# Summing the residual's squares on GpSimd instead of TensorE, for the first token block of each stage boundary

## The chip, the cores and the metric

The kernel runs on one core of one Trainium2 chip. Its metric is the device time of one execution in microseconds. Times of engines come from one profiled execution.

## The reference, cut to what matters

A decoder trunk of two layers over 1040 tokens (16 meta tokens and 1024 real ones), 1024 channels wide: a Mamba-2 mixer with a convolutional feed-forward network, then sliding-window attention over shared keys and values with another such network. Each of the four parts is normed before and after, and added to the residual stream `h`:

```python
def rms_norm(x, w):
    xf = x.astype(jnp.float32)
    y = xf * lax.rsqrt(jnp.mean(xf * xf, axis=-1, keepdims=True) + RMS_EPS)
    return (y * w.astype(jnp.float32)).astype(x.dtype)

for i in range(DEPTH):
    if i < N_A_LAYERS:
        mix = mamba2_mixer(rms_norm(h, a_norm_pre[j]), ...)
        h = h + rms_norm(mix, a_norm_post[j])
    else:
        if j == 0:
            kv = (rms_norm(h, kv_norm) @ w_kv).reshape(...)
        mix = swa_sink_attention(rms_norm(h, b_norm_pre[j]), ...)
        h = h + rms_norm(mix, b_norm_post[j])
    ffn = conv_ffn(rms_norm(h, f_norm_pre[i]), ...)
    h = h + rms_norm(ffn, f_norm_post[i])
```

The change bears on the mean of squares `mean(xf * xf)` of `h` in three of these norms.

## The kernel before, in words

All activations stay on chip, channels on the 128 partitions (8 groups of channels, index `k` or `m`), tokens along the free dimension. The 1040 tokens are cut in three blocks, `BLK`: block 0 with 272 tokens, blocks 1 and 2 with 384. Every projection is done with weights split in a high and a low fp16 half, three matmuls for each product (L1799 to L1801). Weights come through a buffer `stage`; ScalarE makes their high half (`hi`, L691), VectorE the low half (`lo`, L1258), and TensorE waits for `w_lo`.

Between two stages stands a *boundary* `p`: the last tiles of one projection, the post-norm, the addition to `h`, the pre-norm and the first tiles of the next projection overlap, block by block, in the order `ORD = (1, 2, 0)`; the first, second and third block below are meant in this order. Boundary 0 is after the Mamba-2 mixer, 1 after the first feed-forward network, 2 after attention, 3 at the end. `TAIL = (4, 2, 4, 2)` says how many of the 8 output tiles are done block by block, as *tail tiles*. There is no scheduler: each engine has one program written by hand, executed in order, and counting semaphores join them.

The squares of the mixer's output are summed over the 8 channel groups by GpSimd in `T2` (`tail_squares`, L595 the square, L617 the addition, a drain behind each), all but the last tile's, which ScalarE squares into `T1` once `T2` is done (it waits for `mix_sq_summed`; L884 in boundary 0, L886 in the others). TensorE turns the two into a mean over the channels by two products with a matrix of ones (`mean_post`, L1870 and L1872). ScalarE takes the reciprocal root (`rms`, L711 logarithm, L713 exponential), VectorE scales the output and adds it to `h` (`post`, L1274 and L1279, for each `k`), and ScalarE squares the new `h` (`square`, L727, semaphore `h_sq`). The sum over the 8 groups is done here by TensorE with eight accumulating products with ones (`mean_pre`, L1885). ScalarE's `pre` waits for all eight (`h_sq_used`), and VectorE's `pre` (L1292) then makes the normed input of the next projection, whose low halves (L358) are VectorE's and for two of the eight groups GpSimd's (`lows`).

The queues matter. GpSimd in a boundary does the tail squares of the first block, those of the second, the lows of the first, the tail squares of the third, the other lows. ScalarE with four tail tiles (boundaries 0 and 2) has this order, where `close(o1, ...)` ends with the square that waits for GpSimd:

```python
post(p, o0)
squares(q_, o0)
close(o1, tiles[1:])
pre(q_, o0)
```

With two tail tiles (boundary 1) `close(o1, tiles[1:])` comes after `pre(q_, o0)` and the first block's splits. TensorE in boundaries 0 and 2: the first block's tail tiles, one of the second block, `mean_post` of the first, the other three of the second, `mean_pre` of the first, two tail tiles of the third block, `mean_post` of the second, two more tail tiles, then the first two tiles of the next projection for the first block, `mean_pre` of the second, `mean_post` of the third, and the third tile of the next projection.

Of the kernel before, what the change touches and what calls it, by code (L numbers as in the profile page):

```python
# [7 lines left out]
KD = D // P  # L8
# [66 lines left out]
def first_slot(g):  # L75

    return GT + SLOTS * g
# [22 lines left out]
ORD = (1, 2, 0)  # L100
# [4 lines left out]
def block_rank(v, b):  # L105

    return b if v == 0 else ORD.index(b)
# [16 lines left out]
def program(nc, h0, wa, wd, wdt, prm, out):  # L124
    F32, F16 = mybir.dt.float32, mybir.dt.float16
    ALU, ACT, AX = mybir.AluOpType, mybir.ActivationFunctionType, mybir.AxisListType
    ds = bass.ds

    with ExitStack() as ctx:
        def sb(name, shape, dt=F32):  # L130
            return ctx.enter_context(nc.sbuf_tensor(name, shape, dt))

        def sem(name):
            return ctx.enter_context(nc.semaphore(name))
# [14 lines left out]
        onesD = sb("onesD", [P, P])  # L149
# [7 lines left out]
        PS = ctx.enter_context(nc.psum_tensor("PS", [P, 8, 512], F32))  # L157
# [5 lines left out]
        def mix_r1(k, b):  # L163
            s, n = BLK[b]
            return R1[:, ds(k * n + KD * s, n)]
# [14 lines left out]
        def mix_big(k, b):  # L180
            s, n = BLK[b]
            return BIG[:, k, s:s + n]
# [14 lines left out]
        def sq_slot(q, k, b):  # L197

            n = BLK[b][1]
            return AUX[:, 384 * k:384 * k + n] if q == 0 else mix_big(k, b) if q == 3 else mix_r1(k, b)  # L200
# [84 lines left out]
        update_ready, h_new = sem("update_ready"), sem("h_new")  # L285

        h_sq, h_sq_used, pre_rsqrt = sem("h_sq"), sem("h_sq_used"), sem("pre_rsqrt")
        x_normed, xn_hi, xn_lo_v = sem("x_normed"), sem("xn_hi"), sem("xn_lo_v")
        xn_lo_p = sem("xn_lo_p")

# [195 lines left out]
        def _(eng):  # L486
# [98 lines left out]
            def post_squares(p, j0, mix):  # L585
# [34 lines left out]

                return tail_squares

            def boundary(p, q, j0, mix):
                tail_squares = post_squares(p, j0, mix)
                tail_squares(ORD[0])
                tail_squares(ORD[1])
                if q is not None:
                    lows(q, ORD[0])
                tail_squares(ORD[2])
                if q is not None:  # L630
                    lows(q, ORD[1])
                    lows(q, ORD[2])
# [51 lines left out]
        def _(eng):  # L684
# [47 lines left out]

            def pre(q, b):
                s, n = BLK[b]
                eng.wait_ge(h_sq_used, 24 * q + 8 * block_rank(q, b) + 8)
                rms(T1, 2 if q == 0 and b == 1 else 7, s, n, pre_rsqrt, eps)

            def high(v, b, k):
# [243 lines left out]
            for g in range(NG - 1):  # L982
                for s in range(SLOTS):
                    i = first_slot(g) + s
# [26 lines left out]
            for s in range(SLOTS):  # L1011
                i = T_Z3 + s
# [168 lines left out]
            for c, (i, b) in enumerate(Q_SEQ):  # L1181
                s, n = BLK[b]
                eng.wait_ge(acc_ready, 3 * J_Q + c + 1)
                for hh in range(2):
                    r = eng.activation(q_stack(2 * i + hh, s, s + n)[64 * hh:64 * hh + 64],
                                       PS[64 * hh:64 * hh + 64, c % 6, 0:n], ACT.Copy,
                                       scale=1.0 / (WS * AD ** 0.5))
# [604 lines left out]
        def _(eng):  # L1792
# [81 lines left out]
            def mean_pre(q, b):  # L1874

                s, n = BLK[b]
                bank = 2 if q == 0 and b == 1 else 7
                if q == 0 and b == 2:
                    eng.wait_ge(pre_rsqrt, 1)
                elif q > 0:  # L1880
                    eng.wait_ge(pre_rsqrt, 3 * q + ORD.index(b))
                for k in range(KD):
                    i = 24 * q + 8 * block_rank(q, b) + k
                    eng.wait_ge(h_sq, i + 1)
                    eng.matmul(PS[:, bank, 0:n], onesD[:, :], sq_slot(q, k, b), start=(k == 0),  # L1885
                               stop=(k == KD - 1)).then_inc(h_sq_used, 1)

            def boundary(p, q, u0, j0, units, x, u_next, j_next, head_free=None):

# [218 lines left out]
            for g in range(NG):  # L2108
                for s in range(SLOTS):
                    i = first_slot(g) + s  # L2110
# [66 lines left out]
            for c, (i, b) in enumerate(Q_SEQ):  # L2177
# [5 lines left out]
                for k in range(KD):  # L2183
                    if i == 0:
                        wait_low(eng, x_index(3, b, k))
                    r = products(PS[:, c % 6, 0:BLK[b][1]], i % 2, k, x_big, b, k == 0, k == KD - 1)
# [147 lines left out]
```

## Time and profile before

| | us |
|---|---|
| median of 3 runs | 2694.93 (2693.72 to 2696.7) |
| the profiled execution | 2693.99 |
| its span | 2692.3 |
| TensorE busy | 2617.8 (97%) |
| VectorE busy | 1474.7 (55%) |
| ScalarE busy | 946.1 (35%) |
| GpSimd busy | 644.2 (24%) |

In the profile PE is TensorE (PEld its weight loads), DVE VectorE, ACT ScalarE, POOL GpSimd; `POOLq` is GpSimd's sequencer at a semaphore. L1885 is line 1885 of the kernel before. Busy shares are of the whole span, and a busy TensorE need not be on the path: what counts in a boundary is which wait ends last. Starts of matmuls are exact, their ends modelled, and a row of n merged instructions carries their common length. A product with ones of fp32 operands appears as two matmul records. The boundaries with the change lie at 830 to 905 us (0), 1541 to 1620 (1) and 1937 to 2016 (2).

### The profile page before, as it was taken

To read this page: it belongs to the slowest core of one execution; us is meant where nothing else is said; L and a number is where in the kernel's file an instruction comes from. 1 tells how busy PE (TensorE), PEld (TensorE's weight loads), DVE (VectorE), ACT (ScalarE), POOL (GpSimd) and SP (SyncE) were. 2 spreads that over 40 slices of the span, in tenths; PEclk is the share of its full clock that TensorE was granted. 3 is DMA by queue.
4 is the path that set the end of the run, shared out by engine and by line. 5 is a ranking of instruction groups with operands and counts; after the bars stand their busy time and mean duration, and the time that the engine had idled before them with its cause. 6 is when DMAs were issued, how large, how long until landed. Compare 5 with 4: busy or idle time off the path is not lost.

```text
span 2692.3 us, 43939 instructions
## 1 busy us (share of the span) xinstructions
PE 2617.8 (97%) x17942; PEld 1760.4 (65%) x17942; DVE 1474.7 (55%) x1898; ACT 946.1 (35%) x1742; POOL 644.2 (24%) x410
## 2 busy tenths in 40 slices
PE   8799999999999999999999998999999999999998
PEld 5566666666666666666666665676666666666665
DVE  6576676677587754544511267496276554543123
ACT  5333333343233423233211255497353223232121
POOL 1042544444234101100021211054421001001121
PEclk9899999999999999999999998998999999999999
DMA  3111111111131111111111111100111111111111
GB/s 110 39 32 40 32 40 32 32 36 36 32 119 32 40 55 47 50 52 47 59 51 54 48 32 32 48 2 2 47 32 55 49 52 47 54 50 54 54 54 63
DMA packets 38041, 123.93 MB, mean 46 GB/s; under 512 B 3361, under 2 KB 12705, under 8 KB 37921
## 3 DMA queue, kind: packets, MB, share of 16 engines
q1 hardware_dynamic: 37920, 122.25, 14.1%
q8 instruction: 86, 1.41, 0.2%
q14 instruction: 35, 0.28, 0.0%
HBM read 118.04 MB, written 4.19 MB: 45 GB/s over the span
## 4 chain that ended last, share of the span: by engine, by line
PE 87%; DVE 6%; ACT 4%; issue 2%; ACTq 1%; POOL 1%; POOLq 0%; DVEq 0%; DMA 0%
PE PS L1799 25%; PE PS L1800 25%; PE PS L1801 25%; PE PS L2016 2%; PE PS L1885 2%; ACT BIG L1198 1%; PE PS L2023 1%; PE PS L2046 1%; PE PS L2008 1%; DVE UB L1292 1%; ACT BIG L1211 1%; PE PS L2034 1%; PE PS L2066 1%; DVE BIG L1543 1%; DVE TT L1364 0%
## 5 line engine op out<-in xcount | busy, mean ns | idle before, releaser
L1799 PE MATMUL PS<-R,whi 128*128 128x384 f16 (+1 forms) x3168 | 987.0, 312 | 15.3 <-DVE wlo L1258 12.6
L1800 PE MATMUL PS<-R,whi 128*128 128x384 f16 (+1 forms) x3168 | 986.7, 311 | 0.0
L1801 PE MATMUL PS<-R,wlo 128*128 128x384 f16 (+1 forms) x3168 | 986.5, 311 | 0.0
L1258 DVE SCALAR_TENSOR_TENSOR wlo<-stage,whi 128x1024 f16<-128x1024 f32 (+1 forms) x182 | 246.1, 1354 | 733.8 <-ACT whi L691 733.7
L1799 PE MATMUL PS<-BIG,whi 128*128 128x384 f16 (+1 forms) x1452 | 452.2, 311 | 12.2 <-issue 8.3
L1800 PE MATMUL PS<-BIG,whi 128*128 128x384 f16 (+1 forms) x1452 | 452.3, 312 | 0.0
L1801 PE MATMUL PS<-BIG,wlo 128*128 128x384 f16 (+1 forms) x1452 | 452.2, 311 | 0.0
L1799 PEld LDWEIGHTS PS<-R,whi 128*128 128x128 f16 x3168 | 311.2, 98 | 180.1 <-issue 12.9
L1800 PEld LDWEIGHTS PS<-R,whi 128*128 128x128 f16 x3168 | 311.1, 98 | 162.5 <-issue 9.2
L1801 PEld LDWEIGHTS PS<-R,wlo 128*128 128x128 f16 x3168 | 311.2, 98 | 157.1 <-issue 1.0
L638 POOL TENSOR_TENSOR BIG<-TT,BIG 128x1040 f32 x44 | 96.7, 2197 | 799.9 <-ACT BIG L1113 799.9
L691 ACT ACTIVATE whi<-stage 128x1024 f16<-128x1024 f32 (+1 forms) x182 | 199.3, 1097 | 145.8 <-PE PS L1801 138.9
L1354 DVE SCALAR_TENSOR_TENSOR TT<-UB,pr,TT 128x1040 f32<-128x1040 f32 x168 | 218.7, 1302 | 29.3 <-issue 28.0
L521 POOL TENSOR_TENSOR TT<-AUX,upper 128x1024 f16<-128x1024 f16 (+1 forms) x72 | 154.7, 2169 | 256.3 <-PE PS L2046 229.4
L1799 PEld LDWEIGHTS PS<-BIG,whi 128*128 128x128 f16 x1452 | 142.6, 98 | 87.4 <-issue 13.0
L1800 PEld LDWEIGHTS PS<-BIG,whi 128*128 128x128 f16 x1452 | 142.5, 98 | 72.9 <-issue 3.9
L1801 PEld LDWEIGHTS PS<-BIG,wlo 128*128 128x128 f16 x1452 | 142.5, 98 | 72.2 <-issue 1.4
L785 ACT ACTIVATE UB<-PS 128x384 f32<-128x384 f32 (+1 forms) x120 | 54.8, 458 | 285.9 <-PE PS L1801 285.6
L1113 ACT ACTIVATE BIG<-TT 128x1040 f32 (+1 forms) x44 | 47.1, 1070 | 285.8 <-DVE TT L1678 285.8
L595 POOL TENSOR_TENSOR TT<-R 128x384 f32<-128x384 f32 (+1 forms) x63 | 51.3, 831 | 397.9 <-ACT R L705 260.3
L1364 DVE SCALAR_TENSOR_TENSOR TT<-UB,pr,TT 128x1040 f32<-128x1040 f32 x72 | 102.2, 1420 | 73.6 <-ACT TT L793 69.9
L705 ACT ACTIVATE UB<-PS 128x384 f32<-128x384 f32 (+1 forms) x240 | 99.8, 450 | 106.5 <-PE PS L1801 106.5
(240 smaller groups left out, 3189.4 us busy)
## 6 DMA issues: line engine op xcount, KB each, us to landing
stage<-wa SPq DMA_DIRECT2D x164, 512.0 KB, 3.5
stage<-wd SPq DMA_DIRECT2D x32, 704.0 KB, 4.0
hT<-h SPq DMA_DIRECT2D x4, 1536.0 KB, 11.2
out<-hT SPq DMA_DIRECT2D x4, 768.0 KB, 3.9
hT<-h SPq DMA_DIRECT2D x2, 1088.0 KB, 9.9
out<-hT SPq DMA_DIRECT2D x2, 512.0 KB, 2.8
pr<-prm SPq DMA_DIRECT2D x1, 328.0 KB, 6.6
BIG<-wdt SPq DMA_DIRECT2D x1, 128.0 KB, 10.6
```

What stands on the lines that cost most here:

```text
L521: r = eng.tensor_tensor(aU[part][0:T, 0:HG * T].rearrange("p (h l) -> p h l", h=HG), ar_p[part][0:T, ds(g * HG + c * NH, HG)].unsqueeze(2) ...
L638: eng.tensor_tensor(BIGh[:, ds(t, 1), L:2 * L], T2, BIGh[:, ds(t, 1), 0:L], ALU.subtract).then_inc(hid_lo, 1)
L691: eng.activation(WH[slot + 2 * aux][:, 0:width], stage[:, slot, 0:width], ACT.Copy, scale=WS).then_inc(w_hi, 1)
L705: r = eng.activation(dst, PS[:, 3 * st_ + b, 0:n], ACT.Copy, scale=scale)
L785: eng.activation(dst, PS[:, gemm_bank(i, b), 0:n], ACT.Copy, scale=scale).then_inc(evac, 1)
L1258: eng.scalar_tensor_tensor(out=WL[d][:, 0:width], in0=stage[:, slot, 0:width], scalar=WS, in1=WH[d][:, 0:width], op0=ALU.mult, op1=ALU.sub ...
L1354: r = eng.scalar_tensor_tensor(out=dst, in0=cin[:, o:o + L], scalar=prc(col + k), in1=dst, op0=ALU.mult, op1=ALU.add)
L1364: r = eng.scalar_tensor_tensor(out=T0, in0=UB[:, i % 2, o:o + L], scalar=prc(C_AW + (g * GT + j) * CONV_A + k), in1=T0, op0=ALU.mult, op1= ...
L1799: eng.matmul(acc, WH[slot][:, ws], x(0, k, b), start=first, stop=False)
L1800: eng.matmul(acc, WH[slot][:, ws], x(1, k, b), start=False, stop=False)
L1801: return eng.matmul(acc, WL[slot][:, ws], x(0, k, b), start=False, stop=last)
L1885: eng.matmul(PS[:, bank, 0:n], onesD[:, :], sq_slot(q, k, b), start=(k == 0), stop=(k == KD - 1)).then_inc(h_sq_used, 1)
```

## The change

GpSimd gets `residual_squares`, between the tail squares of the first and of the second block, in boundaries 0, 1 and 2. It adds the eight squares of `h` of the first block in two groups of four, each as a tree: two pair additions, a drain, one addition of the pairs' sums. TensorE then takes two products with ones for that block, where it took eight, and waits for `h_sq_sum`. For the second and third block, and for the kernel's first norm, the eight products stay. The semaphore `h_sq_used` counts one for each block after the first norm, and eight for each block in it.

```diff
--- before.py
+++ after.py
@@ -285,6 +285,7 @@
         update_ready, h_new = sem("update_ready"), sem("h_new")
 
         h_sq, h_sq_used, pre_rsqrt = sem("h_sq"), sem("h_sq_used"), sem("pre_rsqrt")
+        h_sq_sum = sem("h_sq_sum")
         x_normed, xn_hi, xn_lo_v = sem("x_normed"), sem("xn_hi"), sem("xn_lo_v")
         xn_lo_p = sem("xn_lo_p")
 
@@ -620,9 +621,23 @@
 
                 return tail_squares
 
+            def residual_squares(q_, b):
+
+                i = 24 * q_ + 8 * ORD.index(b)
+                for half in range(2):
+                    k0 = 4 * half
+                    for k in (k0, k0 + 2):
+                        eng.wait_ge(h_sq, i + k + 2)
+                        eng.tensor_tensor(sq_slot(q_, k, b), sq_slot(q_, k, b), sq_slot(q_, k + 1, b), ALU.add)
+                    eng.drain()
+                    eng.tensor_tensor(sq_slot(q_, k0, b), sq_slot(q_, k0, b), sq_slot(q_, k0 + 2, b),
+                                      ALU.add).then_inc(h_sq_sum, 1)
+
             def boundary(p, q, j0, mix):
                 tail_squares = post_squares(p, j0, mix)
                 tail_squares(ORD[0])
+                if q is not None:
+                    residual_squares(p + 1, ORD[0])
                 tail_squares(ORD[1])
                 if q is not None:
                     lows(q, ORD[0])
@@ -732,7 +747,7 @@
 
             def pre(q, b):
                 s, n = BLK[b]
-                eng.wait_ge(h_sq_used, 24 * q + 8 * block_rank(q, b) + 8)
+                eng.wait_ge(h_sq_used, 8 * (b + 1) if q == 0 else 24 + 3 * (q - 1) + ORD.index(b) + 1)
                 rms(T1, 2 if q == 0 and b == 1 else 7, s, n, pre_rsqrt, eps)
 
             def high(v, b, k):
@@ -1879,11 +1894,18 @@
                     eng.wait_ge(pre_rsqrt, 1)
                 elif q > 0:
                     eng.wait_ge(pre_rsqrt, 3 * q + ORD.index(b))
-                for k in range(KD):
-                    i = 24 * q + 8 * block_rank(q, b) + k
-                    eng.wait_ge(h_sq, i + 1)
-                    eng.matmul(PS[:, bank, 0:n], onesD[:, :], sq_slot(q, k, b), start=(k == 0),
-                               stop=(k == KD - 1)).then_inc(h_sq_used, 1)
+                summed = q > 0 and b == ORD[0]
+                ks = (0, 4) if summed else range(KD)
+                for k in ks:
+                    if summed:
+                        eng.wait_ge(h_sq_sum, 2 * (q - 1) + k // 4 + 1)
+                    else:
+                        eng.wait_ge(h_sq, 24 * q + 8 * block_rank(q, b) + k + 1)
+                    r = eng.matmul(PS[:, bank, 0:n], onesD[:, :], sq_slot(q, k, b), start=(k == 0), stop=(k == ks[-1]))
+                    if q == 0:
+                        r.then_inc(h_sq_used, 1)
+                if q > 0:
+                    r.then_inc(h_sq_used, 1)
 
             def boundary(p, q, u0, j0, units, x, u_next, j_next, head_free=None):
 
```

Order on GpSimd, boundary 0, before: `R` holds the mixer's output and the squares of `h`, `TT` the temporaries `T1` and `T2`. The rows are the last tail tile of the first block, the second block's three, and the first block's lows.

```order
L595 TENSOR_TENSOR TT<-R 128x384 [waits out_b]
L617 TENSOR_TENSOR TT<-TT 128x384
L595 TENSOR_TENSOR TT<-R 128x384 [waits out_b]
L617 TENSOR_TENSOR TT<-TT 128x384
L595 TENSOR_TENSOR TT<-R 128x384 [waits out_b]
L617 TENSOR_TENSOR TT<-TT 128x384
L595 TENSOR_TENSOR TT<-R 128x384 [waits out_b]
L617 TENSOR_TENSOR TT<-TT 128x384
L358 TENSOR_TENSOR R<-BIG,R 128x384 [waits xn_hi] x2
```

The same place after the change (L596 and L618 are the former L595 and L617):

```order
L596 TENSOR_TENSOR TT<-R 128x384 [waits out_b]
L618 TENSOR_TENSOR TT<-TT 128x384
L631 TENSOR_TENSOR R<-R 128x384 [waits h_sq] x2
L633 TENSOR_TENSOR R<-R 128x384
L631 TENSOR_TENSOR R<-R 128x384 [waits h_sq] x2
L633 TENSOR_TENSOR R<-R 128x384
L596 TENSOR_TENSOR TT<-R 128x384 [waits out_b]
L618 TENSOR_TENSOR TT<-TT 128x384
L596 TENSOR_TENSOR TT<-R 128x384 [waits out_b]
L618 TENSOR_TENSOR TT<-TT 128x384
L596 TENSOR_TENSOR TT<-R 128x384 [waits out_b]
L618 TENSOR_TENSOR TT<-TT 128x384
```

Six additions, the first four of which wait for ScalarE's squares of `h`, now stand ahead of the second block's three tail tiles.

TensorE, boundary 0, before: the end of the second block's tail tiles, the first block's products with ones (`onesD`), and the first tail tile of the third block.

```order
L1799 MATMUL PS<-BIG,whi 128x384
L1800 MATMUL PS<-BIG,whi 128x384
L1801 MATMUL PS<-BIG,wlo 128x384
L1885 MATMUL PS<-R,onesD 128x384 [waits h_sq,pre_rsqrt]
L1885 MATMUL PS<-R,onesD 128x384 [waits h_sq] x7
L1799 MATMUL PS<-BIG,AUX 128x272 [waits w_lo,out_b]
```

And after the change:

```order
L1814 MATMUL PS<-BIG,whi 128x384
L1815 MATMUL PS<-BIG,whi 128x384
L1816 MATMUL PS<-BIG,wlo 128x384
L1904 MATMUL PS<-R,onesD 128x384 [waits h_sq_sum,pre_rsqrt]
L1904 MATMUL PS<-R,onesD 128x384 [waits h_sq_sum]
L1814 MATMUL PS<-BIG,AUX 128x272 [waits w_lo,out_b]
```

The place in the order is the same; two products stand for eight, and they wait for GpSimd instead of ScalarE.

## Rows read from the trace of the kernel before

**Rows 1.** Busy time of each engine by stretch: after the busy times, granted clock, DMA, GB/s

```profile
840.00:905.00 65.00, 62.49 (x366) 40.26 (x364) 52.49 (x96) 32.47 (x65) 16.39 (x16) 1.00 0.11 33
905.00:1535.00 630.00, 630.00 (x4295) 419.97 (x4293) 259.44 (x215) 165.96 (x248) 87.20 (x49) 1.00 0.16 52
1535.00:1620.00 85.00, 85.00 (x515) 55.55 (x514) 53.66 (x99) 43.36 (x89) 10.20 (x10) 1.00 0.08 26
```

**Rows 2.** Chain that ended last, boundaries 0 and 1: start us, us, what

```profile
844.25 5.17 PE PS L1885 x16
...
849.45 0.58 ACT TT L711
...
850.65 1.68 DVE BIG L1292 x3
...
1553.91 5.16 PE PS L1885 x16
```

**Rows 3.** Timeline, TensorE: start, us, engine, line, operation, tiles, [idle before, its releaser]

```profile
878.81 0.32 PE L1799 MATMUL PS<-R,whi 128*128 128x384 f16 x1 [1.57 <-DVE wlo L1258]
...
1983.50 0.32 PE L1799 MATMUL PS<-R,whi 128*128 128x384 f16 x1 [1.80 <-ACT UB L1096]
```

**Rows 4.** Timeline, GpSimd, boundaries 0 and 2

```profile
844.56 1.13 POOL L617 TENSOR_TENSOR TT<-TT 128x384 f32<-128x384 f32 x1
...
863.79 0.77 POOL L617 TENSOR_TENSOR TT<-TT 128x272 f32<-128x272 f32 x1
864.71 0.77 POOL L595 TENSOR_TENSOR TT<-R 128x272 f32<-128x272 f32 x1
865.62 0.89 POOL L617 TENSOR_TENSOR TT<-TT 128x272 f32<-128x272 f32 x1
...
1948.88 0.83 POOL L595 TENSOR_TENSOR TT<-BIG 128x384 f32<-128x384 f32 x1 [9.05 <-ACT BIG L888]
...
1950.98 0.82 POOL L595 TENSOR_TENSOR TT<-BIG 128x384 f32<-128x384 f32 x1
```

**Rows 5.** Timeline, ScalarE, boundaries 0, 1 and 2

```profile
841.97 0.99 ACT L727 ACTIVATE R<-hT 128x384 f32<-128x384 f32 x2 [0.48 <-DVE hT L1279]
...
848.06 0.52 ACT L884 ACTIVATE TT<-R 128x384 f32<-128x384 f32 x1 [5.10 <-POOLq L618]
...
1552.07 0.99 ACT L727 ACTIVATE R<-hT 128x384 f32<-128x384 f32 x2 [0.47 <-DVE hT L1279]
...
1947.44 0.99 ACT L727 ACTIVATE BIG<-hT 128x384 f32<-128x384 f32 x2 [0.47 <-DVE hT L1279]
...
1953.09 0.49 ACT L886 ACTIVATE TT<-PS 128x384 f32<-128x384 f32 x1 [3.90 <-POOLq L618]
...
1955.44 0.58 ACT L711 ACTIVATE TT<-PS,eps 128x384 f32<-128x384 f32 x1 [1.48 <-PE PS L1885]
```

**Rows 6.** Timeline, VectorE, boundaries 0 and 1

```profile
863.87 2.02 DVE L1274 SCALAR_TENSOR_TENSOR R<-R,pr,TT 128x384 f32<-128x384 f32 x2
865.82 1.11 DVE L1279 TENSOR_TENSOR hT<-hT,R 128x384 f32<-128x384 f32 x1
866.86 0.61 DVE L1274 SCALAR_TENSOR_TENSOR R<-R,pr,TT 128x384 f32<-128x384 f32 x1
...
1544.43 1.15 DVE L1274 SCALAR_TENSOR_TENSOR R<-R,pr,TT 128x384 f32<-128x384 f32 x2 [25.89 <-ACT TT L713]
1545.49 0.55 DVE L1279 TENSOR_TENSOR hT<-hT,R 128x384 f32<-128x384 f32 x1
1545.97 0.61 DVE L1274 SCALAR_TENSOR_TENSOR R<-R,pr,TT 128x384 f32<-128x384 f32 x1
```

**Rows 7.** Busy time by stretch in the first mixer, columns as in the first group

```profile
52.00:58.00 6.00, 3.08 (x24) 2.03 (x22) 5.38 (x11) 0.91 (x2) 0.00 (x0) 1.00 0.09 13
116.00:120.00 4.00, 1.67 (x11) 0.78 (x8) 3.84 (x4) 1.28 (x2) 0.00 (x0) 1.00 0.00 0
120.00:124.00 4.00, 2.67 (x13) 1.31 (x14) 2.55 (x4) 0.27 (x2) 1.19 (x1) 0.51 0.45 131
```

## The prediction

> **What bounds the kernel now.** I read the table of busy time by stretch first, then the chain of waits through the first boundary, then the engines' timelines at the three boundaries where the change acts. Outside the boundaries TensorE has no idle time worth the name: 630.00 us of 630 between 905 and 1535 us [rows 1]. So whatever a boundary delays or advances TensorE by is the change in the total. The boundary after the state-space mixer is different: TensorE is busy 62.49 us of 65 there, and the one after the first down projection again 85.00 of 85 [rows 1].
>
> The chain says why. TensorE's eight products with ones end at about 849.4 us, ScalarE's logarithm starts at 849.45, VectorE's normalisation of the first block at 850.65, and from there the chain runs through VectorE, ScalarE and GpSimd until TensorE resumes at 878.81, having waited for VectorE's low half of a weight tile [rows 2, 3]. After 850.65 no link of it is a TensorE instruction. In the boundary after attention it is the same: an idle 1.80 us, then TensorE at 1983.50 [rows 3] (the row names a ScalarE copy that was long done by then; by the program this matmul needs the same low half of the third weight tile, so I read it as the same wait). So in these two boundaries (I call them 0 and 2) TensorE's own work before the wait is free by now, and what counts is when VectorE starts the first block's normalisation. In boundary 1 TensorE is the path.
>
> **What is removed.** Eight products take 5.17 us [rows 2], 0.646 each. Six go at each boundary, three boundaries: 3 x 6 x 0.646 = 11.6 us of TensorE work. That is the most that can be won, and only where TensorE sets the end.
>
> **What is added, and where it stands in GpSimd's queue.** At each boundary GpSimd gets six additions of 128x384 with three drains, ahead of its squares of the second block's tail tiles. Those tail squares were done as their tiles came: in boundary 0 the last addition but one began at 844.56 [rows 4] and ScalarE's square of the last tile, which waits for them, ran at 848.06 [rows 5]. Behind that square in ScalarE's queue stands the logarithm of the first block. Now the tail squares start only when the tree is done, and the tree cannot end before the last residual square.
>
> *Length of a GpSimd step.* A square and an addition together, with their drains, have a pitch of 1948.88 to 1950.98 = 2.10 us [rows 4], so an addition step is about 1.1 us, the same as the 1.13 recorded next to VectorE work [rows 4]. After the last residual square come one pair addition and one sum: 2.2 us. Three tail tiles (boundaries 0 and 2) cost 3 x 2.10 = 6.3 us, one (boundary 1) 2.1.
>
> *What the additions do to VectorE.* While the tree runs, VectorE is making the residual out of two on-chip operands, back to back. Before, a GpSimd addition and such VectorE work met at 863.8 to 866.5: two multiplies from 863.87, one addition from 865.82, the next instruction at 866.86, 2.99 us [rows 6]. Undisturbed the same three have a pitch of 1.06 + 0.48 = 1.54 us (1544.43, 1545.49, 1545.97) [rows 6]. So 1.45 us were lost to three GpSimd instructions that are recorded with 0.77 + 0.77 + 0.89 = 2.43 us [rows 4], 60% of their time. For a 384-wide addition of 1.0 us I take 0.6 us. Bounds: nothing (it may fall into gaps), and the full 1.0 us. Four of the six additions fall before the last residual square, so that square is late by 4 x 0.6 = 2.4 us (0 to 4.0).
>
> The Trainium skill (SBUF — State Buffer, "Who interferes with whom") says that a VectorE instruction with two SBUF inputs and a GpSimd instruction that reads SBUF exclude each other for the whole instruction, whoever starts first. The rows agree in kind, not in length: by the rule the loss would be the whole 1.0 us of an addition and the sum +14.15, by the rows 0.6 us and +9.35.
>
> *Boundary 0.* Last residual square ends 841.97 + 0.99 = 842.96 [rows 5]; + 2.4 = 845.35. + 2.2: tree done 847.6. + 6.3: tail squares done 853.9, ScalarE's square at 854.05. The logarithm follows one pitch later (0.43 to 0.45), 854.5, against 849.45: **+5.05 us**. TensorE finished its two products at 848.3, 1.1 us sooner than before, and nobody can use it.
>
> *Boundary 2.* 1947.44 + 0.99 = 1948.43 [rows 5]; + 2.4 + 2.2 + 6.3 = 1959.35, the square at 1959.5 against 1953.09. Then ScalarE's copy and the logarithm at 0.39 each, 1960.3, against 1955.44: **+4.85 us**.
>
> *Boundary 1.* Only one tail tile is left to GpSimd and ScalarE's wait for it comes after the first block's logarithm, so the tail squares hide under some 10 us of products. Last square 1552.07 + 0.99 = 1553.06 [rows 5]; + 2.4 + 2.2 = 1557.7; one product 0.65 and the 0.15 to its end mark: 1558.5, against 1553.91 + 5.16 = 1559.07 [rows 2]: **-0.55 us**. TensorE stands idle from about 1554.4 to 1557.7 in place of six products. With no loss on VectorE it would be -2.95.
>
> Other edits cost nothing: the increments of h_sq_used now come once per block instead of eight times, and the waits for them stand for the same last product; the first norm (q = 0) is as it was.
>
> **Sum.** 5.05 + 4.85 - 0.55 = +9.35 us. The profiled execution took 2693.99 us (span 2692.3 and 1.7 around it), so 2703.3; against the median of the runs, 2694.93, that is 2704.3. I go by the median.
>
> *Bounds.* No loss on VectorE: boundary 0: 842.96 + 2.2 + 6.3 + 0.15 + 0.45 = 852.05, +2.6; boundary 2: +2.45; boundary 1: -2.95; together +2.1, 2697.0. Full loss (4.0 us): each 1.6 more, +14.15, 2709.1.
>
> **Rivals.**
> 1. *The additions slip in beside VectorE* (no loss): +2.1, 2697.0. For it: the additions start as each pair of squares arrives, and VectorE has short gaps. Against: [rows 4, 6]. Chance 0.15.
> 2. *Whole-instruction exclusion*: +14.15, 2709.1. For it: VectorE's addition of 865.82 ends 0.4 us after GpSimd's of 865.62 does, as if it had waited for its end. Against: the mean of 60%. Chance 0.10.
> 3. *TensorE's clock falls in the new idle.* In this trace a stretch with 1.67 us busy of 4 is followed by one at 0.51 of full clock, the lower of the two levels (1.2 against 2.4 GHz); another with 3.08 busy of 6 stayed at 1.00 [rows 7]. The new idle of 3.3 us in boundary 1, and that before the third head tile in boundaries 0 and 2, could do it. One fall costs, where TensorE is the path, half of about 4 us: +2, and two of them +4, on top of the forecast: 2706 to 2708.5. Chance 0.12.
> 4. *The other side: TensorE's saving survives.* If the tree cost VectorE nothing and the tail squares were not behind it, the end of the two products would set all three boundaries: 845.85 against 849.4, 1951.4 against 1955.44, 1555.95 + 0.15 against 1559.07: -3.5, -4.0, -2.95, together -10.5, 2684.5. For it the second block's tail squares would have to be over by 849; with three tiles at 2.10 they would have to start by 842.7, when the tree still lacks its last square. It decides only if ScalarE did not wait for them there. Chance 0.05.
> 5. *The change does not do what it says*, the sums come so early that nothing waits and the boundary keeps its slack: within 0.2% of before. Chance 0.03.
>
> The forecast keeps 0.55, spread from +6 to +12. What a measurement of this kernel can tell from no change is about 0.2%, 5.4 us. Faster by more: 0.05 (rival 4). Within: rivals 1 and 5 and a little of the forecast's lower end, 0.20. Slower by more: 0.75. The range for 8 in 10 leaves out rival 4 and the far end of rival 3: 2696.8 to 2710; the forecast's own is 2701 to 2707.
>
> **What would show it.** In the profile after: GpSimd's new lines between the two groups of tail squares, each addition near 1.0 us; VectorE's residual pairs no longer at 1.0 us but longer by 0.6 for each addition, last residual square of boundary 0 near 845.3 instead of 842.96; ScalarE's square of the last tile released by GpSimd at about 854 and not 848; TensorE's idle before its second product with ones 3 us; TensorE's idle ahead of the third head tile much longer than 1.57 and 1.80 us; the gap between boundary 0 and boundary 1 unchanged. Wrong would be: residual squares at their old pitch (then rival 1), the first block's logarithm in boundaries 0 and 2 no later than before (rival 4), or a span of boundary 1 longer than before (then the clock, or a loss on VectorE above 3 us).

## The result, and the profile after

The changed kernel takes 2707.34 us (median of 5 runs, 2706.68 to 2710.58) against 2694.93 (also 5 runs, 2693.72 to 2696.7; the median of the three ahead of the prediction was the same), a ratio of 1.0048 (1.0036 to 1.0059): slower by 12.4 us, where 9.35 was forecast. That is inside the stated 2696.8 to 2710, and 0.3 us above the forecast's own 2701 to 2707. The span of its profiled execution is 2707.2 us, 14.9 more than before.

The inserted lines shift the numbers. The squares of `tail_squares` L595 and its additions L617 are now L596 and L618; ScalarE's last square is L899 (boundary 0) and L901, its logarithm L726, its residual square L742; VectorE's residual pair L1289 and L1294, its normalisation L1307; TensorE's products with ones L1904. New are GpSimd's pair addition L631 and sum L633.

The chain of waits through boundary 0 of the changed kernel (start, duration, what; [rows 2] before):

```profile
842.49 1.27 DVE R L1289
843.76 1.28 DVE hT L1294
...
845.07 0.53 ACT R L742
...
845.67 1.23 POOL R L631
846.89 1.01 issue
847.90 1.36 POOLq L632
...
849.40 1.13 POOL R L633
...
857.11 0.52 ACT TT L899
...
858.17 0.53 ACT TT L728
...
858.73 1.68 DVE BIG L1307 x3
```

TensorE's products are gone from it. VectorE, the pair additions and sums, then the three pairs of tail squares (left out here, 850.53 to 857.03) lead to ScalarE's last square and the normalisation. The latter starts at 858.73, against 850.65 (2.35 us of the difference arise ahead of the boundary, see below). The timelines of VectorE and GpSimd show how the tree makes its own last input late:

```profile
839.66 1.36 DVE L1289 SCALAR_TENSOR_TENSOR R<-R,pr,TT 128x384 f32<-128x384 f32 x1
840.95 0.54 DVE L1294 TENSOR_TENSOR hT<-hT,R 128x384 f32<-128x384 f32 x1
841.41 0.60 DVE L1289 SCALAR_TENSOR_TENSOR R<-R,pr,TT 128x384 f32<-128x384 f32 x1
841.94 0.55 DVE L1294 TENSOR_TENSOR hT<-hT,R 128x384 f32<-128x384 f32 x1
...
843.69 1.34 DVE L1294 TENSOR_TENSOR hT<-hT,R 128x384 f32<-128x384 f32 x1
...
845.49 1.82 DVE L1294 TENSOR_TENSOR hT<-hT,R 128x384 f32<-128x384 f32 x2
```

```profile
839.38 1.22 POOL L631 TENSOR_TENSOR R<-R 128x384 f32<-128x384 f32 x1 [10.31 <-ACT R L742]
842.12 1.22 POOL L631 TENSOR_TENSOR R<-R 128x384 f32<-128x384 f32 x1 [1.52 <-ACT R L742]
843.49 1.13 POOL L633 TENSOR_TENSOR R<-R 128x384 f32<-128x384 f32 x1
845.67 1.23 POOL L631 TENSOR_TENSOR R<-R 128x384 f32<-128x384 f32 x1 [1.05 <-ACT R L742]
847.94 1.32 POOL L631 TENSOR_TENSOR R<-R 128x384 f32<-128x384 f32 x1 [1.05 <-ACT R L742]
849.40 1.13 POOL L633 TENSOR_TENSOR R<-R 128x384 f32<-128x384 f32 x1
...
855.98 1.00 POOL L618 TENSOR_TENSOR TT<-TT 128x384 f32<-128x384 f32 x1
```

Each of the first four of the tree's six additions makes the VectorE instruction that it meets 0.75 to 0.8 us longer (1.36 against 0.60, 1.34 against 0.55).

ScalarE's last square and the logarithm behind it, boundaries 0 and 2 (before: [rows 5]):

```profile
857.11 0.52 ACT L899 ACTIVATE TT<-R 128x384 f32<-128x384 f32 x1 [9.25 <-POOLq L619]
857.54 0.56 ACT L726 ACTIVATE TT<-PS,eps 128x384 f32<-128x384 f32 x1
...
1969.67 0.49 ACT L901 ACTIVATE TT<-PS 128x384 f32<-128x384 f32 x1 [7.73 <-POOLq L619]
...
1970.43 0.58 ACT L726 ACTIVATE TT<-PS,eps 128x384 f32<-128x384 f32 x1
```

TensorE's instructions after an idle time (before: [rows 3]); 1651.53 is the first one behind boundary 1 that waits, and it stood at 1641.37:

```profile
539.76 1.13 PE L2030 MATMUL PS<-AUX,BIG 128*128 128x512 f32 x2 [2.31 <-ACT hT L858]
850.59 1.65 PE L1904 MATMUL PS<-R,onesD 128*128 128x384 f32 x2 [3.35 <-POOL R L633]
886.87 0.32 PE L1814 MATMUL PS<-R,whi 128*128 128x384 f16 x1 [1.57 <-DVE wlo L1273]
1566.78 1.65 PE L1904 MATMUL PS<-R,onesD 128*128 128x384 f32 x2 [4.15 <-POOL R L633]
1651.53 0.48 PE L1814 MATMUL PS<-BIG,whi 128*128 128x384 f16 x1 [8.27 <-issue]
1963.45 0.91 PE L1904 MATMUL PS<-BIG,onesD 128*128 128x384 f32 x2 [2.84 <-POOL BIG L633]
1998.47 0.32 PE L1814 MATMUL PS<-R,whi 128*128 128x384 f16 x1 [1.86 <-ACT UB L1111]
```

The first row stood at 537.41: 2.35 us are lost before any changed instruction. Of them 1.43 are there at 57.85 us already (that matmul stood at 56.42), with a granted clock of 0.79 from 16 to 24 us where it was 1.00 before, and 2.03 by 93.06 (before: 91.03), with 0.83 from 53 to 63 us, again against 1.00. The last 0.3 come between 123 and 537 us. Such an offset differs from one execution to the next. With the offsets at these rows, and that of the first product with ones of boundary 2 (1959.80 against 1950.08) for the attention, the span divides:

| stretch | forecast | measured |
|---|---|---|
| ahead of the change | 0 | +2.35 |
| boundary 0 (886.87 - 878.81 - 2.35) | +5.05 | +5.71 |
| boundary 1 (1651.53 - 1641.37 - 8.06) | -0.55 | +2.10 |
| attention | 0 | -0.44 |
| boundary 2 (1998.47 - 1983.50 - the rest) | +4.85 | +5.25 |

The three boundaries give +13.06. In boundary 1 a spell of the low clock (a stretch at the lower level, 1.2 GHz, where granted 1.00 is 2.4) stands behind the idle time (busy time by stretch, columns as in [rows 1]):

```profile
1562.00:1567.00 5.00, 0.85 (x3) 0.24 (x3) 1.66 (x2) 1.42 (x3) 3.48 (x4) 0.96 0.01 2
1567.00:1570.00 3.00, 3.00 (x8) 1.34 (x9) 0.33 (x1) 1.10 (x2) 1.50 (x2) 0.50 0.00 0
```

### The profile page after: what moved, and what is told of

Same layout as the page of the kernel before. It is cut to its first block, busy times and chain, and to the rows that moved or that the text cites. A ratio compares the mean times of both kernels' runs of the same rounds, so it can differ in the third digit from the quotient of the medians.

```text
span 2707.2 us, 43891 instructions
## 1 busy us (share of the span) xinstructions
PE 2617.4 (97%) x17906; PEld 1754.1 (65%) x17906; DVE 1483.3 (55%) x1898; ACT 945.8 (35%) x1742; POOL 664.7 (25%) x428
## 4 chain that ended last, share of the span: by engine, by line
PE 85%; DVE 6%; ACT 4%; issue 2%; POOLq 1%; POOL 1%; ACTq 1%; DVEq 0%; DMA 0%
PE PS L1814 25%; PE PS L1815 25%; PE PS L1816 25%; PE PS L2038 2%; PE PS L1904 1%; ACT BIG L1213 1%; PE PS L2045 1%; PE PS L2068 1%; PE PS L2030 1%; DVE UB L1307 1%; ACT BIG L1226 1%; DVE R L1289 1%; PE PS L2056 1%; PE PS L2088 1%; DVE BIG L1558 1%
## 5 line engine op out<-in xcount | busy, mean ns | idle before, releaser
L596 POOL TENSOR_TENSOR TT<-R 128x384 f32<-128x384 f32 (+1 forms) x63 | 51.5, 834 | 358.3 <-ACT R L720 260.3
```

## The experiments

In the expectations Q is my theory: GpSimd's work sets boundaries 0 and 2, by its place in the queue and by what it takes from VectorE, while TensorE is the path in boundary 1. "Before" ran beside each, 2694.9 to 2695.2. The rows stand as recorded; delays in the text have the kernel's own offset, read as in the first row above (537.41 before), taken off. The times of stages are those of one profiled execution each. The diffs are cut to the decisive lines: where the tree stands in fewer or more boundaries, TensorE's products and waits are changed to match.

### The load without the saving

The kernel before, TensorE unchanged at eight products; GpSimd does six additions of the tree's size on constants, at the same waits and place (one drain more; `x0` and `x1` are free stretches of `AUX`).

```diff
+ def like_residual(q_, b):
+     for half in range(2):
+         for k, x_ in ((4 * half, x0), (4 * half + 2, x1)):
+             eng.wait_ge(h_sq, i + k + 2)
+             eng.tensor_tensor(x_, pr[:, 0:384], pr[:, 200:584], ALU.add)
+         eng.drain()
+         eng.tensor_tensor(x0, x0, x1, ALU.add)
+         eng.drain()
  tail_squares(ORD[0])
+ if q is not None:
+     like_residual(p + 1, ORD[0])
```

> The kernel before, with the six GpSimd additions and the drains at the same place of its queue in boundaries 0, 1 and 2, waiting for the same squares, but adding constants into a free stretch of AUX (one drain more, between the two halves). TensorE keeps all its eight products with ones. Theory Q (the queue: ScalarE's wait for the second block's tail squares, which now stand behind the tree on GpSimd, sets the start of the first block's normalisation in boundaries 0 and 2; the VectorE loss beside the additions makes the tree later): both boundaries lose what the changed kernel loses there, +5.7 and +5.2 us, boundary 1 nothing (its products still find their squares in time): 2694.9 + 11 = 2706, between 2704 and 2708. Theory T (the loss comes from TensorE waiting for the sums, and from its clock falling in that wait): no such wait here, so within 2 us of 2694.9. Theory P (only the VectorE loss matters, the queue does not): +2.5 and +3, 2700.

Measured: 2708.74, ratio 1.0048 (1.0034 to 1.0061), the same as the change. TensorE resumes in boundary 0 at

```profile
886.70 0.38 PE L1812 MATMUL PS<-R,whi 128*128 128x384 f16 x1 [1.57 <-DVE wlo L1271]
886.87 0.53 PE L1813 MATMUL PS<-R,whi 128*128 128x384 f16 x1
```

which is 5.75 later than before (offset 2.14); the change has 5.71. Boundary 2 is 5.49 longer, against 5.25. Boundary 1 shows no idle time. But the next matmuls take 0.53 us where 0.33 is their length: a spell of the low clock starts here. At the first matmul behind boundary 1 that waits (1650.94, against 1641.37) the kernel has lost 1.68 us more. The change has no such spell at this place, and loses 2.10 in boundary 1 instead, so that the totals agree is in part chance; that the two boundaries agree is not. The median lies 0.7 above Q's range, theory T's 2695 is far off: in boundaries 0 and 2 the products that the change takes from TensorE are worth nothing, and the load is the whole cost.

The same spell, 9 to 12 matmuls long, stands behind boundary 0's last wait in the profiles of four more runs below (all squares awaited, ScalarE's logarithm first, load behind the tail squares, TensorE kept at work), and costs 1.3 to 1.7 us each time; it is missing in the changed kernel and in the half-width run. What decides whether it falls there is not shown, and it has to be kept in mind where their totals are read.

### The load, half as wide

```diff
- eng.tensor_tensor(x_, pr[:, 0:384], pr[:, 200:584], ALU.add)
+ eng.tensor_tensor(x_, pr[:, 0:192], pr[:, 200:392], ALU.add)
```

> As e1_load_only (the kernel before, with six GpSimd additions on constants in the place of the tree, TensorE unchanged at eight products), but the additions are 192 wide instead of 384. Theory Q (each addition holds VectorE's next instruction up for about as long as the addition works, and the rest is the additions' own length in GpSimd's queue): the last residual square is late by about 1.3 (2.5 in e1_load_only), what follows it in the queue shrinks from 2.1 to about 1.3; boundary 0 +3.5, boundary 2 +3.3, so 2695.2 + 7 = 2702 (2700.5 to 2703.5). Theory W (an addition costs VectorE a fixed price per instruction, whatever its width): the square stays 2.5 late, boundaries +4.7 each: 2704.7 (2704 to 2706). Theory R (GpSimd's queue is all, VectorE loses nothing that counts): boundaries +1.3 each: 2698.

Measured: 2702.36, 1.0028 (1.0016 to 1.0039). VectorE and GpSimd:

```profile
839.51 0.95 DVE L1287 SCALAR_TENSOR_TENSOR R<-R,pr,TT 128x384 f32<-128x384 f32 x1
840.38 0.94 DVE L1292 TENSOR_TENSOR hT<-hT,R 128x384 f32<-128x384 f32 x1
```

```profile
839.22 0.81 POOL L629 TENSOR_TENSOR AUX<-pr 128x192 f32<-128x192 f32 x1 [1.52 <-ACT R L740]
840.17 0.73 POOL L631 TENSOR_TENSOR AUX<-AUX 128x192 f32<-128x192 f32 x1
```

An addition of half the width takes 0.34 to 0.39 us from VectorE (0.95 against 0.61, 0.94 against 0.55), half of 0.75, though GpSimd's own record shrinks only from 1.22 to 0.81. Boundary 0 is longer by 3.79 (882.44, offset -0.16), not 5.75. Q holds; a price per instruction (W) and the queue alone (R) do not.

### The load behind the second block's tail squares

```diff
  tail_squares(ORD[0])
- if q is not None:
-     like_residual(p + 1, ORD[0])
  tail_squares(ORD[1])
+ if q is not None:
+     like_residual(p + 1, ORD[0])
```

> As e1_load_only, with the same six additions of 384, but behind the second block's tail squares in GpSimd's queue, so that neither those nor TensorE wait for them. Theory Q (queue place and VectorE are two prices): the queue place costs nothing now, ScalarE's log in boundaries 0 and 2 stands where it did before; but the additions run at about 848 to 855, beside VectorE's normalisation of the first block, of which four or so meet them at 0.75 us each: boundary 0 and 2 +2 to +3.5 each, 2700.5 (2698.5 to 2702.5). Theory R (the queue place is the whole cost): 2695 (2694 to 2696). Theory V (six additions cost the same wherever they stand, since VectorE is the path all through the boundary): 2706 to 2708.

Measured: 2700.01, 1.002 (1.0011 to 1.0029). The logarithm is back in its place (849.43 without the offset of 2.42, against 849.45), but the normalisation that took 1.68 us for its first three now takes:

```profile
853.05 3.51 DVE L1305 SCALAR_TENSOR_TENSOR BIG<-hT,pr,TT 128x384 f32<-128x384 f32 x3 [4.55 <-ACT TT L726]
```

and TensorE resumes 2.62 later (883.85), in boundary 2 2.03. So in this place the additions cost less than half of the 5.75 and 5.49: the queue place and VectorE are two prices, as Q had it.

### All eight squares awaited before any addition

```diff
- eng.wait_ge(h_sq, i + k + 2)
+ eng.wait_ge(h_sq, i + 8)
```

> The changed kernel, but every pair addition waits for all eight squares, so that none runs beside VectorE's residual updates. Theory Q: the squares are back at their old times (last one 842.96 in the old time of boundary 0, not 845.5), but six additions in a row, 6.8 us, follow the last square instead of 2.5; the tree is done 1.3 us later than in the changed kernel in each of the three boundaries: 2707.3 + 4 = 2711, between 2709 and 2713. Theory P (the loss is VectorE's slower residual): with that loss gone each boundary gains 2.5 to 3 us, 2699 to 2700.

Measured: 2712.1, 1.006 (1.0047 to 1.0074). GpSimd's last sum, offset 1.64:

```profile
850.06 0.99 POOL L633 TENSOR_TENSOR R<-R 128x384 f32<-128x384 f32 x1
```

It ends at 849.4 us without the offset, instead of 848.2, though no addition meets the residual any more, and TensorE resumes in boundary 0 6.65 us later than before, not 5.71: adding as the pairs arrive is the better form, although it slows what it waits for.

### ScalarE's logarithm ahead of the wait

The changed kernel; in boundaries 0 and 2 ScalarE does the second block's last tail tile after `pre` of the first block.

```diff
- close(o1, tiles[1:])
+ close(o1, tiles[1:3])
  pre(q_, o0)
  split_x(q, o0, range(4))
+ close(o1, tiles[3:])
```

> The changed kernel, but in boundaries 0 and 2 ScalarE does the close of the second block's last tail tile (the square that waits for GpSimd's tail squares) after the first block's reciprocal root and its first four splits, not before them. GpSimd's and TensorE's programs are those of the changed kernel, the VectorE loss too. Theory Q: the first block's logarithm now starts when TensorE's two products are done, 849.1 in the old time of boundary 0 against 849.45 before and 854.8 after the change; both boundaries fall back to within 1 us of before, and with boundary 1's +2.1 the kernel takes 2697, between 2695 and 2699, 10 us less than the changed one. Theory P (the VectorE loss): it stays, +2.5 and +3, with boundary 1 2702. Theory T: TensorE's wait for the sums stays too, so no more than 2 us below the changed kernel, 2705.

Measured: 2704.67, 1.0033 (1.0021 to 1.0046): a miss, 7.7 us above Q's number. The logarithm did come early, at 851.65 (849.92 without the offset). But the normalisation now ran beside GpSimd's tail squares:

```profile
852.86 3.04 DVE L1308 SCALAR_TENSOR_TENSOR BIG<-hT,pr,TT 128x384 f32<-128x384 f32 x3 [2.53 <-ACT TT L728]
855.83 1.35 DVE L359 TENSOR_TENSOR R<-BIG,R 128x384 f16<-128x384 f32 x1
```

TensorE resumed at 883.23, 2.7 later than before without the offset of 1.73, where the change has 5.7: the delay of the logarithm is gone, and half of what it was worth came back as VectorE's loss. A spell behind it costs 1.55 and boundary 1 again over 2. I had priced the wait and not what its removal starts beside GpSimd. By its total alone the run would speak for theory T (2705, no more than 2 us below the change); T's reason, the wait for the sums, is ruled out by the two boundaries of the load without the saving, where TensorE never waits for a sum.

### The tree in boundary 1 alone

```diff
- if q is not None:
+ if p == 1:
      residual_squares(p + 1, ORD[0])
```

> The changed kernel with the tree in boundary 1 alone; in 0 and 2 TensorE takes eight products as before. Theory Q: boundary 1 has no tail square in front of the first block's logarithm, so only the wait for the sums counts: 2694.9 + 2.1 as in the changed kernel where the clock fell, about -0.5 where it does not fall: 2694 to 2697.5. Theory S (six products less are six products won where TensorE is the path): -3.9, 2691. In both the boundaries 0 and 2 return to their old length: a loss there of more than 1 us would speak against Q.

Measured: 2697.98, 1.0012 (1.0003 to 1.0021). Boundaries 0 and 2 have their old length to 0.01 us, boundary 1 is 3.0 us longer. TensorE waits in boundary 1, and then works at half speed:

```profile
1559.07 1.65 PE L1904 MATMUL PS<-R,onesD 128*128 128x384 f32 x2 [3.87 <-POOL R L633]
```

```profile
1559.00:1564.00 5.00, 4.93 (x13) 2.31 (x14) 2.04 (x4) 2.47 (x5) 1.80 (x3) 0.50 0.01 2
```

The result lies just above Q's range and 7 above S's number: the boundary in which TensorE is the path loses too.

### TensorE kept at work through the wait

The changed kernel, with six idle products into the bank that the first real one overwrites.

```diff
+ if summed:
+     for _ in range(6):
+         eng.matmul(PS[:, bank, 0:n], onesD[:, :], pr[:, 0:n], start=True, stop=True)
  for k in ks:
```

> The changed kernel, with six idle products (ones by constants, into the same bank, overwritten by the first real product) issued by TensorE ahead of its wait for the tree, so that it works through the time in which it waited (3.35, 4.15 and 2.84 us idle in boundaries 0, 1 and 2). The tree's end stays where it is. Theory C (the clock fall behind the idle time is what boundary 1 loses over the prediction): the fall at 1566.6 for 3.4 us goes, and with it 1.7 to 2 us; boundaries 0 and 2 are as long as before, since TensorE waits further down there: 2707.3 - 1.9 = 2705.4 (2704.3 to 2706.5). Theory N (the fall costs nothing that shows, the idle time alone is the loss): 2707.3 (2706.5 to 2708). Theory L (the six products are themselves in the way): 2708 to 2711, with the first tail tile behind them later than in the changed kernel.

Measured: 2707.64, 1.0051 (1.0038 to 1.0065), no gain; but the trace divides it. Two stretches, at boundary 1 and at the end of boundary 0:

```profile
1563.00:1570.00 7.00, 6.71 (x29) 3.67 (x28) 1.73 (x4) 2.49 (x5) 3.94 (x5) 1.00 0.00 1
883.00:890.00 7.00, 5.43 (x23) 2.64 (x22) 5.86 (x9) 6.12 (x12) 1.19 (x1) 0.76 0.42 144
```

In boundary 1 the clock stays high and TensorE gains 1.5 us on the changed kernel, as theory C said. In boundary 0 the fall near 849.8 (granted 0.50 from 850 to 852 us in the change, 1.00 here), where TensorE had time to spare, is gone, but one stands now at 885.3, where it is the path, and takes 1.7 us back. TensorE resumes 5.72 later than before all the same, as in the change: there its wait for the sums costs nothing. A spell costs by where it lands. I had expected boundary 0 to stay as it was.

### Boundary 1, with the products one half tile later

The tree in boundary 1 alone, and TensorE comes to it after the whole last tail tile of the second block.

```diff
  tail(1, o1, 0, kh)
- if q is not None:
-     mean_pre(p + 1, o0)
  tail(1, o1, kh, kt)
+ if q is not None:
+     mean_pre(p + 1, o0)
```

> The tree stands in boundary 1 alone, and TensorE comes to its two products one half tail tile (about 4.8 us) later, behind the whole of the second block's last tail tile. Run e2_boundary1_only (tree there, products at their old place) had TensorE idle 3.87 us in front of them with a clock fall behind, and came out 2.8 us slower than before. Theory Q (the path theory: TensorE is the path in boundary 1, so the saving counts there once the wait is covered): the tree's late end, 3.9 us behind TensorE's old place, is covered by the half tile; no idle time over 0.3 us at 1555 to 1565 and no clock fall there; six products of 0.65 us are gone and three more microseconds of nothing are added: 0.9985 of before, 2691.3 (2690 to 2693.5). Theory S (fewer products with ones never shorten this kernel, since the queues of ScalarE or the banks end the stage): the idle time shows up further on (in front of the mean of the second block or of the heads) and the time is 2694.5 to 2697. Theory T (the additions' loss on VectorE, 3 us, reaches TensorE here too): idle time in front of the heads, 2694 or more.

Measured: 2694.7, 0.9999 (0.999 to 1.0008), while its profiled execution was the fastest of the eleven, 2690.97. The same kernel again:

> e5_later once more, on another chip, with another profile. Its first runs fell in two groups, 2691.0 to 2692.7 (four, the profiled one among them) and 2694.6 to 2696.7 (seven); e11_earlier_high_tree, with the same tree, stood 4.2 below e10_earlier_high, the same kernel without it. Theory Q (the tree at this place is worth 3 to 4 us, and the upper group are runs with more clock falls in the attention, the place where the profiles differ most): a profile of the upper group shows boundary 1 as in e5_later (no clock fall there, PE idle 0.4 to 0.6) and one to three more spells of 1.2 GHz between 1631 and 1880 us; median 2691 to 2695. Theory H (the upper group loses the saving in boundary 1 itself, by idle time and a clock fall at 1565 to 1590): a profile of it shows that fall.

Measured: 2693.4, 0.9992 (0.9983 to 1.0001), with a profiled execution of 2694.72. The two profiles agree in boundary 1, where the clock stays at 1.00 and no wait for the tree is left. They part in attention. Boundary 1 and one stretch of attention, first profile, then second:

```profile
1556.00:1586.00 30.00, 28.54 (x204) 20.17 (x202) 20.75 (x33) 15.60 (x30) 7.90 (x8) 1.00 0.11 34
...
1752.00:1764.00 12.00, 10.18 (x109) 8.01 (x108) 11.00 (x21) 11.48 (x38) 7.57 (x4) 1.00 0.00 1
```

```profile
1556.00:1586.00 30.00, 28.54 (x204) 20.18 (x203) 20.90 (x34) 15.66 (x30) 7.92 (x8) 1.00 0.11 31
...
1752.00:1764.00 12.00, 10.19 (x78) 7.95 (x75) 10.25 (x17) 8.76 (x29) 5.68 (x3) 0.72 0.00 0
```

Boundary 1 is 1.8 us shorter in both (its last products with ones start at 1608.82 and 1609.05, offsets 0.29 and 0.53, against 1610.33). At 1631 us, without their offsets, they are level; by 1873 the second has lost 3.5 us to the first. At the first products of boundary 2 the lead over the kernel before is 3.3 us in the first profile and gone (-0.2) in the second. TensorE has many short waits in attention, and the two executions differ in the spells of the low clock that fall on them; what decides this is not shown. So the saving is real in boundary 1, and in the medians mostly lost further on.

### Also the second block's tree in boundary 1

As in the section above, with the same tree for the second block, for which TensorE now takes two products too.

```diff
  tail_squares(ORD[2])
+ if p == 1:
+     residual_squares(p + 1, ORD[1])
```

> As e5_later, and in boundary 1 GpSimd also adds the second block's squares as a tree (six additions, behind its last tail tile's squares and ahead of the second block's low halves), so that TensorE takes two products there instead of eight, between the second and third head tile. Theory Q: at that place TensorE is the path and the squares of the second block are done before TensorE arrives; six more products of 0.65 us go: 3.9 below e5_later, 2687.4 (2686 to 2690). Theory S (the additions slow VectorE, which makes the next block's residual and low halves, and the heads of the second block wait for it): idle time of 1 to 4 us in front of the second block's heads, and the same time as e5_later or up to 3 us more.

Measured: 2695.94, 1.0004 (0.9995 to 1.0013); Q's 2687.4 is missed by 8.5. The additions met VectorE's residual of the second block, the low half of a weight tile stands behind it, and TensorE waited for that:

```profile
1586.94 1.21 DVE L1275 SCALAR_TENSOR_TENSOR AUX<-stage,AUX 128x1024 f16<-128x1024 f32 x1
```

```profile
1588.30 0.48 PE L1816 MATMUL PS<-R,AUX 128*128 128x384 f16 x1 [3.67 <-DVE AUX L1275]
```

with the low clock behind it (0.48 for a matmul of 0.33). The 1.8 us that boundary 1 had gained are gone (0.04 is left). That is theory S.

### The wait that the change left alone

The kernel before; ScalarE makes the high half of the third head tile's weights ahead of the last tail tile's square.

```diff
- close(o2, tiles[2:])
+ close(o2, tiles[2:3])
+ turned(KD - 2, o2)
+ hi(u_next + 2)
+ close(o2, tiles[3:])
```

> The kernel before (no tree), with ScalarE's high half of the third head tile's weights in boundaries 0 and 2 issued ahead of the last tail tile's square instead of behind it. TensorE stands idle 0.90 and 1.57 us there in boundary 0 [rows 3] and 1.80 in boundary 2, the latter ones for the low halves of these weights, which wait for this high half, which waits in ScalarE's queue behind GpSimd's squares. Theory Q: the low half is done 1.3 to 1.6 us earlier and TensorE resumes that much earlier in each of the two boundaries: 2694.9 - 3.0 = 2692 (2691 to 2693.3). Theory M (the last square, 1 us later behind the high half, is the next to be waited for): the mean of the third block is 0.5 to 1 later, and 2694 to 2695.5 comes out.

Measured: 2693.52, 0.9994 (0.9985 to 1.0003). Both idle times for the low half are gone; boundary 0:

```profile
877.37 0.69 PE L1876 MATMUL PS<-TT,onesD 128*128 128x272 f32 x2
877.93 0.32 PE L1803 MATMUL PS<-R,whi 128*128 128x384 f16 x1
```

Boundary 0 gains 1.7 us and boundary 2 1.9; the profiled execution lost 2.0 of them in attention, with the granted clock at 0.72 in the same stretch, 1752 to 1764.

The same, and the tree in boundary 1 alone with TensorE's products one half tile later:

> e5_later with the edit of e10_earlier_high. In e5_later's profile TensorE's lead over the kernel before was 3.0 us, yet its runs spread from 2691.0 to 2696.7 with the median at that of before. Theory Q (the two savings add up, and the tree's is worth what the runs show, about nothing in the median): 2692 (2690.5 to 2693), as e10_earlier_high. Theory S (the tree's 3 us do show once the spread is gone): 2689. Theory H (the tree in boundary 1 costs by its clock falls): 2693 to 2695, above e10_earlier_high.

Measured: 2689.29 (2687.85 to 2691.49), 0.998 (0.9971 to 0.9989): faster than both kernels, 4.2 below the same kernel without the tree. The granted clock at 1752 to 1764 is 1.00 here, as in the kernel before. The medians do not add up from parts (-0.2 or -1.5 for the tree alone, -1.6 for the order alone, -5.8 for both). The boundaries do: in the profiles the order gains 1.7 and 1.9 and the tree 1.8, together about 5.5, and here the three boundaries gain 1.7, 1.8 and 1.9. So it is the two single edits whose gain is missing, and attention's spells are where the profiles differ; only one or two executions of each were profiled, so that this explains the medians is likely and not shown.

## Why the prediction was right

*What bounds boundaries 0 and 2: right.* There the load without the saving cost as much as the change (5.75 and 5.49 against 5.71 and 5.25), and TensorE's products had left the chain. One sign did not come: TensorE's idle time ahead of the third head tile was to be much longer than 1.57 and 1.80 us, and is 1.57 and 1.86. The delay reached TensorE ahead of that wait: in boundary 0 it sat idle 3.35 us for the sum and 1.06 more at 875.70, and ran at a granted clock of 0.54 from 852 to 857 us.

*The queue: right.* After the tree 6.5 us of tail squares (850.49 to 856.98; 6.3 forecast) stand ahead of ScalarE's last square, and the logarithm is 0.43 behind it.

*VectorE's loss: right in kind, a little small.* 0.75 to 0.8 us for an addition against 0.6 forecast and 1.0 by whole-instruction exclusion. The rows that it came from had additions 272 wide: 1.45 us lost to three of them, scaled by width to 384, is an estimate of 0.68 for each, nearer than the 0.6 that came of their recorded length. Four losses are 3.1 us. The last residual square is late by 3.0 in boundary 2 and by 3.1 in boundary 1, where 2.4 was forecast, and by only 2.55 in boundary 0: there VectorE's first two multiplies met a tail square before and took 1.68 us together, and 1.15 now. Most of what is left of the excess in boundary 0 are the last two additions, 2.7 us from the last square to the tree's end and not 2.2, for they met VectorE's work on the second block (1.32 and 1.13). The Trainium skill (SBUF — State Buffer, "Who interferes with whom") has the whole instruction excluded. The loss is less than the addition's length, 0.75 of about 1.0 us, and the half-width run shows that it goes with the width, 0.75 to 0.37, and not with the length recorded on GpSimd, 1.22 to 0.81. That does not rule an exclusion out. At its undisturbed pitch of 0.53 (841.41 to 841.94) VectorE's multiply ahead of 840.95 began at 840.42, where the addition is recorded until 840.60; in the half-width run it began at 839.85, and the addition is recorded until 840.03. Both fit a VectorE that is held up until 0.18 us before the recorded end. And the addition began at 839.38, when VectorE's previous instruction (839.20 to 839.75) still ran, so its first 0.28 us took nothing from VectorE. What fails is the step from "excluded" to "1.0 us lost".

*Boundary 1: wrong by 2.65 us.* The failing term is the 1558.5 at which TensorE was to be done, against 1559.07 before: its products were put at full speed behind an idle time of 3.3 us. The idle time was 4.15, since VectorE lost 3.1 and not 2.4, and the clock fell, which had been rival 3 at 0.12. With the wait filled, 1.5 us of it came back; the rest is the tree's late end (the second product could start at 1558.7 without the offset, not at 1557.7). The prediction had named both for the case that boundary 1 came out longer: the clock, or a VectorE loss above 3 us. Both were there.

*The total.* 13.06 in the three boundaries against 9.35. Of the 3.7 between them 2.65 are boundary 1; the median was 3.0 above the forecast. 2707.34 lies in rival 3's 2706 to 2708.5 and just outside the forecast's own range: what came is the forecast's mechanism, with small terms too low everywhere and one fall of the clock that counted. In the three boundaries no errors cancelled.

## What to carry to other kernels

Ask of a saving on the busiest engine whether that engine is in the chain of waits at that very place: in two of three places here it was not, and a load put on an engine that was busy 24% of the time cost 5 to 6 us in each of them. Give the load two prices, what stands behind it in its queue and what it takes from an engine that works beside it (here 0.75 us of VectorE's time for each addition), and when a wait is removed, look at what then starts beside the load. Where a gain of a few microseconds shifts a later stretch with many short waits, measure there too: of 1.8 us, 3.3 were there further on in one profile and nothing in another.

## What was not expected of the hardware

- The 192-wide addition took 0.34 to 0.39 us from VectorE and the 384-wide one 0.75 to 0.8, the latter whether it read constants or the squares.
- TensorE's idle time of 3.87 us in front of the second product was followed by the granted clock 0.50, the lower level, at 1559 to 1564 in one run, and that of 4.15 us by 0.50 at 1567 to 1570 in the changed kernel; with products in the place of the latter it was 1.00 at 1563 to 1570. In boundary 2 of the changed kernel it was idle 2.84 us, and the clock stayed at 1.00 from 1960 to 1966.
- Two profiled executions of one kernel, level to 0.1 us at 1631 us (offsets taken off), differed by 3.5 us at 1873, with 1.00 against 0.72 granted at 1752 to 1764.
